# A delta-rule trunk: lower products ahead of the token copies, and two sets of masks behind the doubling steps

## The reference, cut to what matters

```
def step(S, inp):
    r_t, k_t, v_t, w_t, kk_t, a_t = inp
    sa = einsum('bhvk,bhk->bhv', S, -kk_t)
    S = S * w_t + sa[..., None] * (kk_t * a_t) + v_t[..., None] * k_t
    return S, einsum('bhvk,bhk->bhv', S, r_t)
```

## Time and profile before

| | |
|---|---|
| median of 3 runs | 2808.72 us (2807.89 to 2815.1) |
| profiled execution | 2807.61 us |
| its span, first to last instruction | 2805.9 us |
| mean granted TensorE clock | 0.975 of full |
| TensorE busy | 2636.4 us, 94% |
| VectorE busy | 1134.1 us, 40% |
| ScalarE busy | 684.6 us, 24% |
| GpSimd busy | 1378.5 us, 49% |

### The profile page before, as it was taken

One profiled execution on the slowest core, in us unless ns is written; L12 is line 12 of the kernel. 1 busy time (PEld: TensorE's weight loads), 2 busy tenths in 40 slices (PEclk: granted clock), 3 DMA queues, 4 the chain that ended last, 5 costly groups with the idle time before them and its releaser, 6 DMA issues.

```text
span 2805.9 us, 66257 instructions
## 1 busy us (share of the span) xinstructions
PE 2636.4 (94%) x25812; PEld 2496.3 (89%) x25812; DVE 1134.1 (40%) x1758; ACT 684.6 (24%) x1196; POOL 1378.5 (49%) x1179
## 2 busy tenths in 40 slices
PE   5999999999999899999989999999999998999997
PEld 5889889898899899999978898988988898999996
DVE  4535535345246421114445353452453554111244
ACT  3323213223133111112232132231332322110122
POOL 4435346154246545556653461552543564555564
PEclk9999999999999999999989999999999999999998
DMA  5112122022136322212321221221212452222122
GB/s 175 58 52 96 46 74 94 26 89 71 36 100 213 105 68 90 90 53 82 107 83 46 75 85 35 85 76 36 101 55 67 138 163 82 86 90 90 53 79 82
DMA packets 84542, 233.61 MB, mean 83 GB/s; under 512 B 12176, under 2 KB 16288, under 8 KB 83312
## 3 DMA queue, kind: packets, MB, share of 16 engines
q1 hardware_dynamic: 66672, 188.40, 20.7%
q10 hardware_dynamic: 14112, 29.63, 2.8%
q0 software_dynamic: 3552, 12.56, 1.3%
HBM read 198.57 MB, written 31.98 MB: 82 GB/s over the span
## 4 chain that ended last, share of the span: by engine, by line
PE 76%; DVE 11%; PEld 4%; issue 3%; ACT 2%; DMA 1%; POOL 1%; SPq 0%; DVEq 0%; ACTq 0%; PEldq 0%; POOLq 0%
PE psP L639 41%; PE psQ L639 14%; PE psQ L703 10%; PEld psP L639 3%; PE psQ L696 3%; PE psQ L978 2%; PEld psQ L639 1%; PE psQ L951 1%; PE psP L968 1%; PE psP L703 1%; DMA W<-in_w_br 1%; DVE BIG L1555 1%; DVE BIG L1504 1%; PE psQ L943 1%; PE psP L962 1%
## 5 line engine op out<-in xcount | busy, mean ns | idle before, releaser
L639 PE MATMUL psP<-HH,WS 128*128 128x272 f32 x4256 | 871.4, 302 | 54.1 <-DVE BIGR L1478 19.9
L497 POOL TENSOR_SCALAR WS<-W 128x512 fp32r<-128x512 f32 (+1 forms) x392 | 294.2, 751 | 901.7 <-PEq L633 496.8
L639 PEld LDWEIGHTS psP<-HH,WS 128*128 128x128 f32 x4256 | 654.4, 192 | 90.4 <-issue 45.6
L639 PE MATMUL psP<-HH,WR 128*128 128x272 f32 x2240 | 471.9, 293 | 0.0
L639 PE MATMUL psP<-HL,WS 128*128 128x272 f32 x2240 | 471.5, 292 | 0.0
L499 POOL TENSOR_TENSOR WR<-W,WS 128x512 fp32r<-128x512 f32 x280 | 391.0, 1396 | 23.4
L639 PEld LDWEIGHTS psP<-HL,WS 128*128 128x128 f32 x2240 | 360.5, 193 | 0.0
L639 PEld LDWEIGHTS psP<-HH,WR 128*128 128x128 f32 x2240 | 359.8, 194 | 0.0
L703 PE MATMUL psQ<-BIG 64*64 64x64 f32 (+1 forms) x5696 | 275.5, 232 | 42.2 <-DVE BIG L1661 15.9
L639 PE MATMUL psQ<-HH,BIGR 128*128 128x272 f32 x1760 | 305.5, 287 | 0.0
L703 PEld LDWEIGHTS psQ<-BIG 64*64 64x64 f32 x5696 | 220.6, 134 | 89.4 <-issue 72.8
(11 more groups left out here) (270 smaller groups left out, 3301.8 us busy)
## 6 DMA issues: line engine op xcount, KB each, us to landing
W<-in_w_stage SPq DMA_DIRECT2D x88, 512.0 KB, 3.7
W<-in_w_f SPq DMA_DIRECT2D x88, 512.0 KB, 3.6
W<-in_w_gate SPq DMA_DIRECT2D x48, 512.0 KB, 3.8
W<-in_w_f SPq DMA_DIRECT2D x88, 256.0 KB, 2.6
gates_waiting<-GB ACTq DMA_DIRECT2D x48, 272.0 KB, 4.2
BIG<-gates_waiting SPq DMA_DIRECT2D x48, 272.0 KB, 3.0
W<-in_w_br SPq DMA_DIRECT2D x48, 256.0 KB, 2.7
W<-in_w_out SPq DMA_DIRECT2D x16, 512.0 KB, 3.6
```

What stands on the lines that cost most here:

```text
L497: pool.tensor_scalar(high, src, 1.0, 0.0, ALU.mult, ALU.add).then_inc(high_part[q], 1)
L639: mm = pe.matmul(out[:, a, 0:HT], a_, x_[:, a * HT:(a + 1) * HT], start=(first and n == 0), stop=(last and n == 2))
```

## The change

The lower products `L0` to `L2` are made right behind `score2`, ahead of `B_vt` and `tok`, and stand there in the list of jobs. On VectorE the masks `N16` stand behind each score, `L16` behind each lower product, and `TT` behind all of these. `LO32` is made behind the sums of `I2`, and `LO64` behind those of `I3`, each for all three groups and after a wait for `tok2`, whose products still read `BT` and `KT`.

```
-SMALL_A = ([f"score{g}" for g in GR] + ["B_vt"] + [f"{n}{g}" for n in ("tok", "L") for g in GR]
+SMALL_A = ([f"score{g}" for g in GR] + [f"L{g}" for g in GR] + ["B_vt"] + [f"tok{g}" for g in GR]
...
+                    for g in GR:
+                        b = job(f"L{g}")
+                        for i in range(PER):
+                            c = PER * g + i
+                            mm = heads(b[:, 0, HD * i:HD * i + HD], AR[:, c, 0], BT[:, c])
+                        filled(f"L{g}", mm)
                     value_tokens("B", UB[:, 3 * TOK:])
                     for g in GR:
                         b = job(f"tok{g}")
...
-                    for g in GR:
-                        b = job(f"L{g}")
-                        for i in range(PER):
-                            c = PER * g + i
-                            mm = heads(b[:, 0, HD * i:HD * i + HD], AR[:, c, 0], BT[:, c])
-                        filled(f"L{g}", mm)
...
                         emptied_by(f"score{g}", ins)
+                        after(f"score{g}")
+                        tt(N16[:, c:c + 3], NR[:, c:c + 3, 0:HD], bc(K["m16"][:], 1, 3), ALU.mult).then_inc(S["n16"], 1)
                     for g in GR:
...
                         emptied_by(f"L{g}", ins)
-                        after(f"score{g}")
                         after(f"L{g}")
-                        tt(N16[:, c:c + 3], NR[:, c:c + 3, 0:HD], bc(K["m16"][:], 1, 3), ALU.mult).then_inc(S["n16"], 1)
                         tt(L16[:, c:c + 3], LF[:, c:c + 3], bc(K["m16"][:], 1, 3), ALU.mult).then_inc(S["l"], 1)
-                        tt(LO32[:, c:c + 3], LF[:, c:c + 3], bc(K["m32"][:], 1, 3), ALU.mult)
-                        tt(LO64[:, c:c + 3], LF[:, c:c + 3], bc(K["m64"][:], 1, 3), ALU.mult).then_inc(S["lo"], 1)
+                    for g in GR:
+                        c = PER * g
                         dve.wait_ge(S["n16"], it * GROUPS + (g + 1))
                         tt(TT[0][:, c:c + 3], N16[:, c:c + 3], bc(K["eye64"][:], 1, 3), ALU.add).then_inc(S["t1"], 1)
...
+                        if use in ("I2", "I3"):
+                            after("tok2")
+                            for g in GR:
+                                c = PER * g
+                                if use == "I2":
+                                    tt(LO32[:, c:c + 3], LF[:, c:c + 3], bc(K["m32"][:], 1, 3), ALU.mult)
+                                else:
+                                    tt(LO64[:, c:c + 3], LF[:, c:c + 3], bc(K["m64"][:], 1, 3), ALU.mult).then_inc(S["lo"], 1)
                         if use == "M2":
```

## The result

| | before | changed |
|---|---|---|
| median | 2808.3 us (4 runs, 2803.55 to 2815.1) | 2775.28 us (4 runs, 2773.85 to 2785.14) |
| profiled execution, its span | 2807.61, 2805.9 us | 2773.85, 2772.2 us |
| mean granted TensorE clock in it | 0.975 | 0.981 |

The ratio is 0.989, with a 95% interval of 0.9873 to 0.9908. The kernel is 33 us faster where 16 were forecast: twice as much, and outside the range.

The account below looks back on a forecast made before the run. TensorE was taken as the bound, 94% busy, with 27.3 us of waits in reach; 11.4 us of new idle left 15.9, taken as 16, so 2791.6 us profiled, 2792 beside the median, range 2786 to 2799.

Parts of the forecast that it names:

- The path: Whole kernel: TensorE busy 94% of the span; time is won where it idles or the chain runs on VectorE.
- The wait at L1: TensorE at L1, waiting for score2 to be emptied: idles 0.97 us a stage instead of 0.65.
- LO32 met GpSimd's subtraction: VectorE behind the second doubling step: LO32 is held until about 326.9, done 0.5 us before I3's sum; costed at nothing.
- The gain reached the end: Next stage's first fill: the VectorE chain it waits for moves up too, so all of the gain is carried.
- The sum: TensorE from score2 to I1: new idle 11.4 us over 8 stages against 27.3, gain 15.9, taken as 16 us.
- the work laid end to end: Same stretch, timed job by job: 2.2 us a stage, 17.6 in all; the difference from 16 kept for the range.
- the waits did not move: Rival at L1, L2, B_vt and tok0: handovers add up to the old 3.4 us, time stays 2808; chance 0.08.
- the late masks were not late: Rival at I3 and I4: six late masks held by GpSimd at 1.43 us each, 23 us slower, 2831; chance 0.03.
- The clock: Rival in each layer's first stage: the long wait brought the lower clock; shorter waits win 2.9 us, 2789; chance 0.08.
- The drops may as well land the other way: Clock rival's worse case: one more drop in each stage, 12 us, gives 2804; chance 0.05.
- The argument I held against a link: Against the clock rival: clock 0.57 at 256 to 260 with TensorE fully busy; five stages waited as long without a drop.
- The range: Whole kernel, 8 in 10: 2786 to 2799 us, from gains of 11 and 19.5 us and part of either clock case.

Follow-up runs that it names:

- the third experiment: Changed kernel with LO32 and LO64 moved from behind the doubling steps to the sums with the unit matrix, behind L2's mask: 2772.8 us, ratio 0.9876.
- work in place of the pause: Changed kernel with seven of nine chunks' I1 products made twice, 56 more products a stage: 2798.89 us, ratio 0.9969.
- the pads: Unneeded VectorE instructions at each stage's start: changed kernel 2781.15 (two), 2801.11 (four), smaller ones 2778.04 and 2778.92 us; kernel before, one small, 2805.92 us.
- experiment 4: Changed kernel with the pause put back: unit-matrix sums wait for the token copies, I1's second group for all three sums: 2806.89 us, ratio 0.9994.
- experiments 8 and 9: Changed kernel with N16 put back beside L16, behind the lower products, run twice: 2787.48 us (ratio 0.9931) and 2788.56 us (ratio 0.993).
- experiment 3: Changed kernel with LO32 and LO64 beside the sums with the unit matrix instead of behind the doubling steps: 2772.8 us, ratio 0.9876.

## Why the prediction was wrong

**What held.** The path was read rightly. The pauses fell from 27.3 us to 8.0 listed and some 3 in gaps too short for the list; 11.4 was worked out. The wait at L1 is 1.0, as forecast. tok0 and I1 start without a wait. I1 ends 18.4 us behind the second stage's first fill step (294.78 to 313.2). LO32 met GpSimd's subtraction and was covered, by 0.54 and 0.72 us. LO32 and LO64 cost nothing at either late place, as the third experiment shows. The gain reached the end: without the clock's cost the spans differ by 16.7 us in one pair of profiles and 12.2 in another, and the stretch is 2.3 us a stage shorter, 18 in all. The sum said 16, and the work laid end to end 17.6, which came nearer. Neither of the other two priced rivals came: the waits did not move, and the late masks were not late.

**What failed: the clock's term.** The step is the rival "The clock", and the sum that left it out. It gave 0.08 to a gain, and priced that gain by the two stages where a drop stood right behind the pause, 2.9 us. Both drops did go. But the count fell by seven more, four within the stages and three outside them, at places that the change does not touch, and the term was worth some 15 us (13 to 21 by the readings above) instead of 0, the forecast, or 2.9, the rival. "The drops may as well land the other way" was the error: it took the drops as falling by chance, so that their expected change was nothing. The pause put back brought their number back (12 within the stages, after 5), and over the fourteen kernels the clock goes along with how much TensorE pauses, with the exceptions named below.

The argument I held against a link was that TensorE was busy for 4.00 of 4.00 us at 256 to 260 with a clock of 0.57, and that five stages paused as long without a drop there. Both are true, and neither excludes a link that acts later: the pause put back brought drops at other places of the stages as well. The rule named there from the Trainium skill (TensorE: Matmul & The Clock Gate, HAM oscillation), that idle gaps let the clock fall, agrees with the first stages (4.68, 4.53 and 4.18 us with the pause, 3.22 without). The waits in that section's example are for transfers and longer than the 2.1 us here, and it does not explain why the drops stand mostly elsewhere.

**The range** went wrong with it. It took the two ends of the pauses, 11 and 19.5 us, and a part of one small clock case. The profile of the kernel before showed 24 stretches at the lower clock and 47 us of cost, three times the forecast gain, and these were treated as fixed. A range that let a quarter of them go or come would have reached 2780; to hold 2775 it had to let 17 of the 47 us go.

**What stays open.** Which pause or which sparse stretch brings which drop is not settled. Two kernels stand off the line: N16 beside L16 lost 8 us of clock for 4 us of small pauses, and work in place of the pause lost clock though it did not pause more at that place. The stage's length is a rival that is not excluded: no run made the stages longer without a pause or more products, for the pads that should have were taken up by slack or turned into a pause. Against length alone stands N16 beside L16, whose stretch is only 0.13 us longer. A theory that holds all fourteen was not found.

## What to carry to other kernels

Where TensorE is the bound and its clock falls now and then, count the stretches at the lower level first and sum what they cost; a change that removes pauses is worth its pauses and may, as here, be worth nearly as much again in clock, and one that adds small pauses may cost three times their length, so the range has to hold both. Put short masks, which another engine is waited for, ahead of the point where GpSimd starts its next pair, and let those that are read late stand anywhere behind. Take the clock's cost out of the spans before saying where time went, and take more than one profile of a kernel: two of the same kernel still differ by 2.6 and 4.5 us here. When a pad is to make a stage longer, read from the trace that it did before drawing on its result.

## What the runs showed of the hardware that was not expected

A pause of 1.9 us a stage cost 31 us over eight stages where it stood for 15 (experiment 4). Two pauses of 0.2 and 0.3 us a stage cost 12 us, twice (experiments 8 and 9), with 12 and 13 stretches at the lower clock within stages instead of 5. A sum of VectorE over 128x192 float32 elements took 1.44 us instead of 0.34 beside a subtraction of GpSimd of 1.27 us (experiment 3). The mean granted clock is a property of a kernel more than of an execution: 0.9759 to 0.9765 for the kernel before in four series of 17 or 18 executions, 0.981 in both series of the changed kernel.
